# The end of four output projections: two weight blocks taken chunk by chunk, and one rounding moved

## The reference

```python
f = swiglu(rmsnorm(h, ffn1_g_pre), ffn1_w_gu, ffn1_w_down)
h = h + 0.5 * rmsnorm(f, ffn1_g_post)
m = hybrid_mixer(rmsnorm(h, mix_g_pre), mix_w_in, ..., mix_w_out)
h = h + rmsnorm(m, mix_g_post)
c = memory_cross_attention(rmsnorm(h, mem_g_pre), rmsnorm(mem, mem_g_kv), mem_w_q, mem_w_kv, mem_w_o)
h = h + rmsnorm(c, mem_g_post)
f = swiglu(rmsnorm(h, ffn2_g_pre), ffn2_w_gu, ffn2_w_down)
h = h + 0.5 * rmsnorm(f, ffn2_g_post)
```

## Time and profile before

| | us |
|---|---|
| median of 3 runs | 1285.77 (1280.09 to 1289.13) |
| the profiled execution, whole | 1279.41 |
| its span, first to last instruction | 1277.7 |
| TensorE busy | 1229.2, 96% of the span |
| ScalarE, GpSimd, VectorE busy | 443.5, 484.7, 407.1 |
| mean granted TensorE clock | 0.979 of full speed |

### The profile page before, as it was taken

The page is one execution under the profiler, slowest core; times in us unless marked ns, Lnnn a source line. Parts: engine busy times, 40 slices in busy tenths (PEclk is TensorE's granted clock), DMA queues, the critical chain, the costliest instruction groups (busy, mean ns, idle before and its releaser), DMA issues.

```text
span 1277.7 us, 15296 instructions
## 1 busy us (share of the span) xinstructions
PE 1229.2 (96%) x5659; PEld 997.9 (78%) x5659; DVE 407.1 (32%) x708; ACT 443.5 (35%) x668; POOL 484.7 (38%) x218
## 2 busy tenths in 40 slices
PE   8999999999999999899998899699999999999997
PEld 5888888888887677677777787577888888888886
DVE  5531313110017354555335525512713131210004
ACT  4432323231134454344333533323523233231122
POOL 5444353544433332113133751133353535354441
PEclk9999999999998999999897999898999999999999
DMA  5233223332221221112022441012232333322221
GB/s 162 91 99 98 90 93 97 99 99 99 94 88 65 66 83 50 50 51 82 2 82 79 146 138 66 17 51 82 78 92 95 98 99 99 99 98 89 93 82 66
DMA packets 83318, 108.74 MB, mean 85 GB/s; under 512 B 8687, under 2 KB 53837, under 8 KB 83277
## 3 DMA queue, kind: packets, MB, share of 16 engines
q1 hardware_dynamic: 83120, 108.14, 26.8%
q10 hardware_dynamic: 156, 0.04, 0.0%
HBM read 106.06 MB, written 2.10 MB: 85 GB/s over the span
## 4 chain that ended last, share of the span: by engine, by line
issue 40%; PE 36%; POOL 18%; DVE 3%; ACT 1%; DMA 1%; POOLq 0%; SPq 0%; DVEq 0%; ACTq 0%
POOL w_lo L553 17%; PE bank L1384 12%; PE bank L1388 11%; PE bank L1385 11%; PE bank L1404 1%; DMA raw<-in_ffn_w_gu 1%; DVE prob L1084 0%; PE bank L1411 0%; DVE f_fin L1369 0%; DVE tmp L1143 0%; DVE qm_lo L1151 0%; ACT w_hi L605 0%; ACT pt_hi L798 0%; PE bank L1640 0%; DVE pt_lo L1110 0%
## 5 line engine op out<-in xcount | busy, mean ns | idle before, releaser
L553 POOL TENSOR_TENSOR w_lo<-raw,w_hi 128x1024 fp32r<-128x1024 f32 x196 | 473.6, 2426 | 759.6 <-ACT w_hi L605 759.4
L1384 PE MATMUL bank<-xh,w_hi 128*128 128x512 f32 x992 | 392.6, 396 | 8.6 <-ACT xh L618 6.3
L1388 PE MATMUL bank<-xl,w_hi 128*128 128x512 f32 x992 | 387.9, 391 | 0.1
L1385 PE MATMUL bank<-xh,w_lo 128*128 128x512 f32 x992 | 387.9, 391 | 0.0
L605 ACT ACTIVATE w_hi<-raw 128x1024 fp32r<-128x1024 f32 x196 | 203.8, 1054 | 387.1 <-DMA raw<-in_ffn_w_down 168.6
L1384 PEld LDWEIGHTS bank<-xh,w_hi 128*128 128x128 f32 x992 | 187.2, 189 | 53.1 <-issue 11.3
L1388 PEld LDWEIGHTS bank<-xl,w_hi 128*128 128x128 f32 x992 | 187.1, 189 | 40.8 <-DVE xl L944 1.3
L1385 PEld LDWEIGHTS bank<-xh,w_lo 128*128 128x128 f32 x992 | 187.3, 189 | 37.1
L1384 PE MATMUL bank<-mid_hi,w_hi 128*128 (+1 forms) x352 | 138.8, 394 | 0.0
L1388 PE MATMUL bank<-mid_lo,w_hi 128*128 (+1 forms) x352 | 138.0, 392 | 0.0
L1385 PE MATMUL bank<-mid_hi,w_lo 128*128 (+1 forms) x352 | 136.6, 388 | 0.0
(11 more groups left out here) (230 smaller groups left out, 1271.1 us busy)
## 6 DMA issues: line engine op xcount, KB each, us to landing
raw<-in_ffn_w_gu SPq DMA_DIRECT2D x176, 256.0 KB, 3.0
raw<-in_ffn_w_down SPq DMA_DIRECT2D x88, 256.0 KB, 2.9
raw<-in_mix_w_in SPq DMA_DIRECT2D x48, 256.0 KB, 2.8
raw<-in_mem_w_kv SPq DMA_DIRECT2D x32, 256.0 KB, 3.3
raw<-in_mix_w_out SPq DMA_DIRECT2D x16, 256.0 KB, 3.1
raw<-in_mem_w_q SPq DMA_DIRECT2D x16, 256.0 KB, 3.0
raw<-in_mem_w_o SPq DMA_DIRECT2D x16, 256.0 KB, 2.9
x_tok<-in_x SPq DMA_DIRECT2D x4, 512.0 KB, 5.0
```

The costliest lines, as they stand in the source:

```text
L553: gp.tensor_tensor(w_lo[:, n % SLOTS, :], raw[:, n % SLOTS, :], w_hi[:, n % SLOTS, :].bitcast(F32), ALU.subtract).then_inc(lo_ready, 1)
L1384: pe.matmul(dst, w[0], x[0], start=start, stop=False, skip_group_check=loose)
L1385: pe.matmul(dst, w[1], x[0], start=False, stop=False, skip_group_check=loose)
L1388: return pe.matmul(dst, w[0], x[1], start=False, stop=stop, skip_group_check=loose)
```

## The change

The last two blocks of each output projection are no longer done one after the other. `closing_out` waits for both blocks, then goes through the banks: for each m the three matmuls of the last block but one and the three of the last, both into bank m. Banks complete every six matmuls and not every three. In the last bank, between its first three and its last three matmuls, stands the token sum of `acc`, which stood behind the products before. The buffer of the last block but one is given back (`w_used`) only in that last bank. To take two blocks out of the loop of the swiglus, it makes four turns and three blocks are written out behind it. In ScalarE's list the rounding of the third block behind the boundary is no longer ahead of the root; it is done by the next `round_to`, in `pre` after c = 3 at the first and third boundary, and straight behind the copy of the spread root (`rinv`) at the second. At the fourth there is no such block.

```diff
@@ post_norm (ScalarE)
-                round_to(OUT_END[s] + 3)
                 act.wait_ge(fstat, s + 1)
@@ token_sums, out_stat (TensorE)
-            def token_sums(dst, parts):
+            def token_sums(dst, parts, first=True, last=True):
...
-                                         start=n == t == 0, stop=n == len(parts) - 1, skip_group_check=True)
+                                         start=first and n == t == 0, stop=last and n == len(parts) - 1,
+                                         skip_group_check=True)
...
                 token_sums(out_bank(s, 0), [
-                    (fsq(DC - 2), [(f0_saved, s + 1), (fsq_ready, DC * s + DC - 1)]),
-                    (acc, [(facc_ready, F_ADDS * (s + 1))]),
-                    (fsq(DC - 1), [(fsq_ready, DC * (s + 1))])]).then_inc(fstat, 1)
+                    (fsq(DC - 2), [(fsq_ready, DC * s + DC - 1)]),
+                    (fsq(DC - 1), [(fsq_ready, DC * (s + 1))])], False).then_inc(fstat, 1)
@@ new (TensorE)
+            def closing_out(s, n, x):
+
+                w = [weights(n - 1), weights(n)]
+                for m in range(DC):
+                    cols = slice(m * P, (m + 1) * P)
+                    for j in range(2):
+                        last = three(out_bank(s, m)[:, :], (w[j][0][:, cols], w[j][1][:, cols]), x[j],
+                                     False, j == 1, True)
+                        if m == DC - 1:
+                            last.then_inc(w_used, 1)
+                            if j == 0:
+                                token_sums(out_bank(s, 0), [
+                                    (acc, [(f0_saved, s + 1), (facc_ready, F_ADDS * (s + 1))])], True, False)
+                    if m < DC - 1:
+                        last.then_inc(out_done, 1)
@@ swiglu (TensorE)
-                with pe.Fori(0, (FC - 2) // 4) as i:
+                with pe.Fori(0, (FC - 6) // 4) as i:
...
+                for k in range(FC - 5, FC - 2):
+                    pe.wait_ge(midl_done, first + 1 + k)
+                    out_block(s, down + k, hidden(k), False, False)
                 pe.wait_ge(midl_done, first + FC)
-                out_block(s, down + FC - 1, hidden(FC - 1), False, True)
+                closing_out(s, down + FC - 1, (hidden(FC - 2), hidden(FC - 1)))
                 out_stat(s)
@@ mixer (the same in memory, with s = 2, MO blocks and y_l of the memory heads)
-                for c in range(4, DC):
+                for c in range(4, DC - 2):
                     pe.wait_ge(y_l, Y_FOX + c - 3)
-                    out_block(1, B_OUT + c, (xh[:, c, :], xl[:, c, :]), False, c == DC - 1)
+                    out_block(1, B_OUT + c, (xh[:, c, :], xl[:, c, :]), False, False)
+                pe.wait_ge(y_l, Y_GLA)
+                closing_out(1, B_KV - 1, [(xh[:, c, :], xl[:, c, :]) for c in (DC - 2, DC - 1)])
```

More of the change, by code:

```diff
@@ L1403, in token_sums @@
                     for t in range(TC):
-                        last = pe.matmul(dst[:, t:t + 1], square[:, t * P:(t + 1) * P], ones[:, 0:1],
-                                         start=n == t == 0, stop=n == len(parts) - 1, skip_group_check=True)
-                return last
+                        done = pe.matmul(dst[:, t:t + 1], square[:, t * P:(t + 1) * P], ones[:, 0:1],
+                                         start=first and n == t == 0, stop=last and n == len(parts) - 1,
+                                         skip_group_check=True)
+                return done
             def spread(dst, src):
@@ L1884, in memory @@
                 free = {3: (pt_l, N_UNITS), 5: (y_l, Y_GLA + 7), 6: (y_l, Y_GLA + DC)}
-                for c in range(DC):
+                for c in range(DC - 2):
                     pe.wait_ge(y_l, Y_GLA + c + 1)
-                    out_block(2, B_MO + c, (xh[:, c, :], xl[:, c, :]), c == 0, c == DC - 1,
+                    out_block(2, B_MO + c, (xh[:, c, :], xl[:, c, :]), c == 0, False,
                               free={} if c else free, ms=range(DC) if c else range(3, DC))
+                pe.wait_ge(y_l, Y_GLA + DC)
+                closing_out(2, B_UP2 - 1, [(xh[:, c, :], xl[:, c, :]) for c in (DC - 2, DC - 1)])
                 out_stat(2)
```

## The result

| | before | changed |
|---|---|---|
| median us | 1281.14 (8 executions) | 1289.43 (8 executions, 1285.71 to 1294.55) |
| ratio, 95% interval | | 1.0054 [1.0027, 1.008] |
| profiled execution, its span | 1279.41, 1277.7 | 1294.55, 1292.8 |
| mean granted clock, profiled | 0.979 | 0.969 |
| the same kernels once more, median us | 1283.8 (20) | 1291.03 (9), ratio 1.0061 [1.0034, 1.0087] |

The change costs 0.5 to 0.6%, 7 to 8 us: the sign of the forecast, two to three times its +2.75. That 1289.43 lies so near the 1288.5 forecast is owed to the median before, which was 1281.14 over all executions and not 1285.77; the difference is what counts.

A forecast was written before the change was run, and what follows sets the result against it. TensorE, busy 96% of the span, was taken as the bound. Terms -0.6 + 0.1 + 1.35 + 1.9 + 0 = +2.75 us on the 1285.77 median gave 1288.5; range 1280 to 1294.

The forecast's parts named there:

- The moved sum: `acc` sum inside the last bank: about -0.2 us at each of the first three boundaries, +0.1 at the fourth.
- Does the `acc` part wait? ... 0.4 to spare: In the last bank, the sixth chunk's square and add were to finish 0.4 us before the `acc` sum: no wait.
- the first of the signs of being wrong: A TensorE wait for `acc` in the last bank would show the forecast wrong; no size given.
- The third block's subtraction: In the pre-norms, a second GpSimd subtraction stops VectorE: +1.35 us behind the first boundary, +1.9 behind the third.
- Behind the second boundary: Two subtractions in a row there: VectorE's waiting op is let in between them, so TensorE loses 0.
- The rival of the kept port: GpSimd keeps the port for its second subtraction behind the second boundary: +2.4 us more, 1290.9; chance 0.15.
- Both blocks at once: `closing_out` needs the last block's low part 5.5 us earlier; 3.5 to spare, so no cost.
- late buffer: Third block's fetch goes out about 0.7 us before the products end, not 5.5; covered behind the first two boundaries.
- The clock: Half-clock falls around the boundaries: 0.7 us a boundary either way, taken as 0.
- The fourth rival: Clock falls early because sums enter the stream before the products end: +6.9 us on top, 1295.4; chance 0.05.

The follow-up runs named there:

- experiment 9: Changed kernel, second block's rounding moved behind the sixth square, third block's right behind the root; 1285.00 us, ratio 1.0006 against before.
- experiment 3: Also squares_first: changed kernel, rounding of the second block behind the boundary moved from ahead of the squares to behind the sixth; 1287.29 us, ratio 1.0020 against before.
- 2: Also close_only: changed kernel with the third block's rounding put back ahead of the root; 1287.10 us, ratio 1.0040 against before.
- 8: Also sum_behind: changed kernel with the `acc` sum put back behind all products; 1288.31 us, ratio 1.0040 against before.
- experiment 1: Also round_only: kernel before, with only the third block's rounding taken from ahead of the root; 1286.09 us, ratio 1.0019 against before.
- 5 to 7: Kernel before plus, behind first and third boundaries, a GpSimd multiply, five GpSimd memory sets, or two ScalarE copies; once each: 1285.22, 1281.90, 1280.11 us.
- experiment 4: Also squares_first_round_ahead: experiment 3 with the third block's rounding also back ahead of the root; 1286.62 us, ratio 1.0034 against before.

## Why the forecast was right in sign and short in size

**The moved sum: right.** It costs the products 0.8 where it stands (381.58 to 382.38 in the kernel of experiment 9) and 0.09 on the next one; with 1.95 from M to root at full clock that is 2.84 against 3.10, -0.26 at a boundary for -0.2 foreseen. In the profiled execution of the changed kernel parts at half clock hide that: M to root is 2.81, 2.99 and 2.22. At the fourth, M comes 0.9 later (343.58 for 342.69 from the third statistic on) and the root 0.9 nearer (3.67 for 4.56): 0.0 for +0.1.

**"Does the `acc` part wait? ... 0.4 to spare": wrong, the step that failed.** It costed the sixth chunk's square and add from that chunk's own products, as if the earlier squares were done. But banks now complete from 1.4 us behind the pair's start on, and the squares stand behind a rounding in ScalarE's list that waits for a transfer, whose subtraction then stops the first add. The pair doubled the time in which banks complete, to 11 us, and the squares began only 3.5 to 4.7 us behind the first bank; the adds behind them then ran back to back up to the sum. Measured: 0.65, 1.08 and 2.28, together +4.0 in place of 0. It is the first of the signs of being wrong that the forecast named. Shown by experiment 3 (cause taken away, wait gone), by 2 (there without the moved rounding) and by 8.

**The third block's subtraction: right.** +1.35 and +1.9 foreseen, +1.40 and +1.96 measured by itself in experiment 1. That it is GpSimd's reading of SBUF and not the load of the engines is shown by 5 to 7. The stopped ops were of other sizes than foreseen: 1.88 and 2.89 where one of 2.29 stood, +1.75 by themselves for 2.3. But VectorE also idled 0.33 ahead of the first, and from one `xl` to the third behind it took from 396.26 to 409.23 in experiment 1 and from 395.45 to 406.26 before: 2.16 lost, close to the 2.3.

**Behind the second boundary: right.** TensorE's wait for `tmp` was 1.8 (1.75 before). The second subtraction stopped the next `h` but one for 2.13 (705.89), and TensorE didn't wait for that. The rival of the kept port didn't come. **Both blocks at once, late buffer: right**; the latter with experiment 4's reason.

**The clock: open.** At the first boundary it fell at 383.7 in the profiled execution and the last part took 1.84; in the six other profiled executions with the pair it fell at 385.8 or later. Those seven all ran over 20 us at half clock between the first statistic and the second M (20.5 to 27.3), the five without the pair 10.2 to 13.7. The fourth rival's early fall didn't come as it was priced: in none of the seven did the clock fall more than 0.1 us ahead of M at the first three boundaries. But it fell sooner behind M where TensorE had waited for `acc`: after 0.7, 0.5 and 1.5 us in the profiled execution of the changed kernel and 2.6, 0.0 and 1.1 in the next, after 3.5, 2.0 and 3.4 in experiment 3 without the waits, and 5.1, 2.9 and 2.2 before. Over all executions the mean clock is 0.9732 and 0.9721 changed, and 0.9738 before, worth 0.6 to 1.7 us by the slope. Whether the change brings that about, and how, no experiment here settles.

**The sum again.** -0.8 for three tails, 0.0 at the fourth, +3.4 in the pre-norms, and +4.0 for `acc`: +6.6. Measured: 1.0054 and 1.0061 of 1281 to 1284 are +6.9 and +7.8, at an equal clock +5.8 and +6.5. Leaving terms out gives close_only +3.2 (measured +2.9), squares_first +2.6 (+2.5), round_only +3.4 (+2.2, with an error of 1.0), and experiment 9, with both out, -0.8 + 1.6 for the stopped `h` = +0.8 (+0.5). Two don't fit so well: sum_behind (3.4 + 0.9 - 0.3 = 4.0 from its stages, +2.4) and squares_first_round_ahead (4.8 of late roots less 0.8, +2.0). Adding up stages gives up to 2 us too much where a root is late; why isn't shown.

So the gain was real and small, 0.8 us, and without its two costs the change is worth no time that can be measured.

## What to carry to other kernels

When a loop's end is made to deliver its results over a longer time, look up what stands first in the list of the engine that takes them: a wait for a transfer there lets the first results lie, and the work meant to overlap is done in a heap at the end. Slack must be worked out from the start of the consumer's whole list and not from the last operation's own input. And a step of GpSimd that reads SBUF has to be placed by what VectorE does at that moment: GpSimd was idle for 62% of the span, and the same step was free in one place and cost 1.4 to 2 us in another.

## What the runs showed of the hardware

- A VectorE operation with two SBUF inputs was stopped by GpSimd operations that read SBUF (1.10 to 2.89 us in place of 0.68 to 0.75), also by a multiply with a broadcast column, and not by memory sets (0.68). That the reading is what decides agrees with the Trainium skill's page "SBUF — State Buffer", section "Who interferes with whom".
- Where two such GpSimd operations are queued back to back, the waiting VectorE operation ended inside the second (at 401.78 in 398.47 to 404.03), and the next VectorE operation with two SBUF inputs was stopped by the second. So the waiting operation was let in between the two, here, behind the multiply, behind the sets and behind the second boundary.
- Executions of one kernel differ by about 1% with the clock: 56.7 us at half clock in the profiled execution before, 81.7 in the one after, 76.1 in the next of the same kernel. A 2 us effect is seen in a stage of the trace and hardly in the whole time.
